# Starting the converted weight slots half a 16-byte line later in SBUF

## The chip, the cores and the metric

The kernel runs on one core of one Trainium2 chip. The metric is device time of one execution in microseconds. Three runs of the kernel before gave 966.22, 966.21 and 966.04 us, with a median of 966.21 us. The profiled execution has a span of 963.2 us from its first to its last instruction.

## The reference

The input is a sequence of 256 tokens with 1024 features, in float32. Three layers act on it one after another:

- an HGRN2 layer (a projection of 1024 to 4096 columns, a chunked gated recurrence over 8 heads, an output projection) and a squared-ReLU MLP of width 4096;
- a differential-attention layer with shared keys and values and a relative bias, and a second MLP of the same kind;
- a layer that mixes low-rank attention with a short gated convolution (three taps), a gated SiLU MLP of width 2816, and a sigmoid gate on a projected side input.

Every layer has RMS norms before and after its parts. In time it is nearly all matrix products of the form

```python
u = jax.nn.relu(h @ w_up)
return (u * u) @ w_down
```

with about 163 MB of float32 weights that are each read once.

## The kernel before, in words

**Precision scheme.** Each float32 weight and each float32 activation is split in a high part (rounded to the type fp32r, which the multiplier takes in one pass) and a low part (the rest). A product is then three fp32r matmuls: high times high, high times low, low times high. So each piece of weights is loaded into TensorE's array several times.

**Weight stream.** Weights come as "units" of 256 output columns, each in two parts of 128 x 1024 numbers (4 KB per partition). SyncE issues one DMA per part into `w_raw` (4 slots). ScalarE copies `w_raw` to `w_hi` (line 1424, rounding to fp32r). VectorE subtracts and writes `w_lo` (line 1990). `w_hi` and `w_lo` have 5 slots each (line 116). TensorE reads them in `quantum`, `high_records` and `low_records`. The semaphores `hi_ready`, `lo_ready` and `w_used` order this: a conversion waits for a slot that TensorE has done with, and SyncE's next load waits for the low part.

**Matmuls.** Mostly the weights are the stationary operand (128 columns for each load) and the activations (`xs`, `us`, `xs_b`, `xs_m`, `xs_s`) are streamed past them, 256 columns at a time (lines 657, 660, 609, 610, 617, 676 to 678, 682 to 684) or 512 at a time, high and low half together (line 649). In a few units ("tok", lines 689 to 691 and 695 to 697) the activation is stationary and the weights are streamed. Each matmul instruction has its own weight load (LDWEIGHTS) in front of it. The loads run ahead, beside the matmul before them.

**SBUF addresses.** Everything lies at hand-made addresses, one tensor after another, each rounded up to 64 bytes, from a base that is a multiple of 64. The order is `w_raw` (16,384 bytes per partition), `w_hi` (20,480), `w_lo` (20,480), `h`, a gap of 64 bytes, `xs`, a gap of 64 bytes, `mo`, `sq` and the rest, and last an arena in which the tensors of the layers (such as `us`) overlay each other. With respect to a period of 128 bytes `w_raw`, `w_hi` and `w_lo` begin at 0, and `xs` and the arena at 64, counted from the base. Each slot (4096 bytes) and each weight tile (512 bytes) is a whole number of such periods.

**Around the stream** there are RMS norms between the layers (`sums`, two or one true float32 matmuls), the recurrence's level products (lines 904 to 936, true float32), attention score products, and transposes (such as lines 843, 882, 1046).

Of the kernel before, what the change touches and what calls it, by code (L numbers as in the profile page):

```python
# [9 lines left out]
F32R = mybir.dt.float32r  # L10
# [7 lines left out]
P = 128  # L18
# [97 lines left out]
RAWS, SLOTS = 4, 5  # L116
QCOLS = 1024
HALF_PERIOD = 64
OTHER_BANKS = [PAIR0[x] + 2 for x in ("up0", "b_out", "up1", "out2", "gu", "pg")]


def pset_of(p):
    return 3 if p in OTHER_BANKS else p % 2

# [104 lines left out]
def layered_kernel(nc, a, out):  # L229

    ctx = ExitStack()
    with ctx:
# [3 lines left out]
        def sb_at(name, shape, dt, at):  # L236
            return nc.alloc_sbuf_tensor_at(name, shape, dt, offset=at)

        def sb(name, shape, dt=F32):
            size = 4 * int(np.prod(shape[1:]))  # L240
            t = sb_at(name, shape, dt, top[0])
            top[0] += (size + 63) // 64 * 64
            return t


        w_raw = sb("w_raw", [P, RAWS, QCOLS])
        w_hi = sb("w_hi", [P, SLOTS, QCOLS], F32R)
        w_lo = sb("w_lo", [P, SLOTS, QCOLS], F32R)
        h = sb("h", [P, KT, S])
        top[0] += HALF_PERIOD  # L250
        xs = sb("xs", [P, KT, 2 * S], F32R)
        top[0] += HALF_PERIOD
        mo = sb("mo", [P, KT, S])
# [207 lines left out]
        def wait(e, s, v):  # L461
            if not isinstance(v, int) or v > 0:
                e.wait_ge(s, v)
# [136 lines left out]
        def _(pe):  # L600
# [141 lines left out]
            def stream(name, x, kinds=("feat",), per=1, pairs=4, body_pairs=2, last_kt=KT - 1, waits=None,  # L742
# [6 lines left out]
                def body(i):  # L749
# [6 lines left out]
                    for b in range(body_pairs):  # L756
                        pr = i * body_pairs + b + p0
                        pset = pset_of(pr)

                        if pr - 2 in OTHER_BANKS:  # L760
                            wait(pe, pair_summed, pr - 3)
# [2297 lines left out]
```

How the kernel before makes its waits and increments, by code:

```python
        def wait_tile(e, r, t):  # L457
            e.wait_ge(h_tile, KT * r + t + 1)
# [1 line left out]
        def wait(e, s, v):  # L461
            if not isinstance(v, int) or v > 0:
                e.wait_ge(s, v)
# [11 lines left out]
        @block.sync  # L475
# [45 lines left out]
            def i_and_g(i):
                for j in range(2):
                    for part in range(2):
                        load("i0", (2, i), j, part, rows(a["a_w_in"][0], 4 * P * part, 4, 256 * (2 * i + j) + 2 * D, 256))
            times(4, i_and_g)
            square("a_out", a["a_w_out"][0], 4)
            square("up0", a["mlp_w_up"][0], 16)
            deep("down0", a["mlp_w_down"][0])
            sp.wait_ge(rel_out, 16)
            sp.wait_ge(w_used, 2 * UNIT0["up0"])
            sp.dma_start(hankel[:, :, :], bass.AP(rel_dram.tensor, rel_dram.offset, [[1, P], [REL, 16], [1, S]]))\
                .then_inc(hankel_in, 16)
# [48 lines left out]
                                 rows(a["w_down_2"][0], (8 * j + 4 * part) * P, nk, 256 * (2 * i + half), 256),  # L583
                                 nk * 256)
            times(2, down2)
            square("pg", a["w_ple_gate_2"][0], 4)
            for m in range(2):
                sp.wait_ge(row_copied[0], m + 1)
                sp.dma_start(out[0, m * P:(m + 1) * P, 0:512], rowbuf[:, m, 0:512]).then_inc(out_done, 16)
            sp.wait_ge(row_copied[2], 1)
# [3 lines left out]
            sp.wait_ge(row_copied[2], 2)  # L594
            sp.dma_start(out[0, P:S, 768:D], rowbuf[:, 1, 768:D]).then_inc(out_done, 16)
            sp.wait_ge(out_done, 80)
```

## Time and profile before

| | |
|---|---|
| median of three runs | 966.21 us |
| span of the profiled execution | 963.2 us |
| difference of the two (what lies around the span) | 3.0 us |
| TensorE matmul busy | 952.3 us (99%), 7530 instructions |
| TensorE weight load busy | 909.1 us (94%), 7530 instructions |
| VectorE busy | 748.2 us (78%) |
| ScalarE busy | 547.7 us (57%) |
| DMA | 173 GB/s mean |
| granted TensorE clock | full speed in all 40 slices |

Busy time of an engine is the union of its instructions. For matmuls it says only that one or more were under way: they are pipelined, each lasts 276 ns or more, and a new one starts every 113 ns or so. What a matmul costs is therefore read from the distance between two starts, not from its duration.

### The profile page before, as it was taken

To read this page: it belongs to the slowest core of one execution; us is meant where nothing else is said; L and a number is where in the kernel's file an instruction comes from. 1 tells how busy PE (TensorE), PEld (TensorE's weight loads), DVE (VectorE), ACT (ScalarE), POOL (GpSimd) and SP (SyncE) were. 2 spreads that over 40 slices of the span, in tenths; PEclk is the share of its full clock that TensorE was granted. 3 is DMA by queue.
4 is the path that set the end of the run, shared out by engine and by line. 5 is a ranking of instruction groups with operands and counts; after the bars stand their busy time and mean duration, and the time that the engine had idled before them with its cause. 6 is when DMAs were issued, how large, how long until landed. Compare 5 with 4: busy or idle time off the path is not lost.

```text
span 963.2 us, 18430 instructions
## 1 busy us (share of the span) xinstructions
PE 952.3 (99%) x7530; PEld 909.1 (94%) x7530; DVE 748.2 (78%) x1129; ACT 547.7 (57%) x819; POOL 89.4 (9%) x91
## 2 busy tenths in 40 slices
PE   9999999999999999999999999999999999999998
PEld 8999999999999998999999999999999999999998
DVE  6998778978855599867987844489887998787777
ACT  6652366656454476756665544455666665556455
POOL 5334101000201000001000201001001000000000
PEclk9999999999999999999999999999999999999999
DMA  8733444766666836436476575626636467665651
GB/s 256 243 120 115 143 128 140 218 200 197 195 183 193 267 109 197 150 113 183 136 215 197 176 214 184 194 68 182 183 110 202 127 197 214 187 190 170 203 175 44
DMA packets 164723, 166.62 MB, mean 173 GB/s; under 512 B 6784, under 2 KB 162832, under 8 KB 164640
## 3 DMA queue, kind: packets, MB, share of 16 engines
q1 hardware_dynamic: 162752, 163.47, 55.5%
q0 software_dynamic: 1056, 1.19, 0.5%
q8 instruction: 60, 0.98, 0.4%
q10 hardware_dynamic: 832, 0.79, 0.4%
q14 instruction: 23, 0.19, 0.1%
HBM read 163.82 MB, written 1.08 MB: 171 GB/s over the span
## 4 chain that ended last, share of the span: by engine, by line
PE 82%; DVE 12%; issue 2%; ACT 2%; DMA 2%; SPq 0%; POOL 0%; ACTq 0%; DVEq 0%
PE ps L657 19%; PE ps L660 16%; PE ps L649 13%; DVE w_lo L1990 4%; PE ps L676 3%; PE ps L677 3%; PE ps L678 3%; PE ps L682 2%; PE ps L683 2%; PE ps L684 2%; PE ps L689 2%; PE ps L609 2%; PE ps L617 2%; PE ps L690 2%; PE ps L691 2%
## 5 line engine op out<-in xcount | busy, mean ns | idle before, releaser
L1990 DVE TENSOR_TENSOR w_lo<-w_raw,w_hi 128x1024 fp32r<-128x1024 f32 (+4 forms) x314 | 375.0, 1205 | 116.1 <-ACT w_hi L1424 110.3
L1424 ACT ACTIVATE w_hi<-w_raw 128x1024 fp32r<-128x1024 f32 x298 | 313.3, 1056 | 200.3 <-PE ps L660 47.6
L657 PE MATMUL ps<-xs,w_hi 128*128 128x256 f32 x1012 | 132.6, 277 | 0.0
L657 PEld LDWEIGHTS ps<-xs,w_hi 128*128 128x128 f32 x1012 | 127.0, 188 | 4.5
L660 PE MATMUL ps<-xs,w_lo 128*128 128x256 f32 x832 | 112.2, 277 | 0.0
L660 PEld LDWEIGHTS ps<-xs,w_lo 128*128 128x128 f32 x832 | 102.9, 188 | 0.2
L682 PE MATMUL ps<-xs,w_hi 128*128 128x256 f32 x320 | 91.4, 285 | 0.4 <-DVE w_lo L1990 0.4
L683 PE MATMUL ps<-xs,w_hi 128*128 128x256 f32 x320 | 89.3, 279 | 0.0
L684 PE MATMUL ps<-xs,w_lo 128*128 128x256 f32 x320 | 89.3, 279 | 0.0
L649 PE MATMUL ps<-xs,w_hi 128*128 128x512 f32 x326 | 85.1, 393 | 0.3 <-DVE mo L2018 0.2
L1431 ACT ACTIVATE tmp<-ps 128x512 f32<-128x512 f32 x75 | 44.5, 593 | 70.6 <-PE ps L649 62.6
L657 PE MATMUL ps<-us,w_hi 128*128 128x256 f32 x626 | 81.9, 277 | 0.0
L657 PEld LDWEIGHTS ps<-us,w_hi 128*128 128x128 f32 x626 | 78.6, 188 | 2.8
L2018 DVE TENSOR_TENSOR mo<-ps,tmp 128x512 f32<-128x512 f32 x75 | 51.6, 688 | 37.1 <-ACT tmp L1431 37.0
L2968 POOL TENSOR_TENSOR sq<-sq 128x512 f32<-128x512 f32 x12 | 20.1, 1676 | 546.0 <-ACT sq L1482 375.6
L660 PE MATMUL ps<-us,w_lo 128*128 128x256 f32 x516 | 69.3, 277 | 0.0
L649 PEld LDWEIGHTS ps<-xs,w_hi 128*128 128x128 f32 x326 | 56.6, 188 | 9.8 <-DVE mo L2018 1.5
L660 PEld LDWEIGHTS ps<-us,w_lo 128*128 128x128 f32 x516 | 63.6, 188 | 0.0
L682 PEld LDWEIGHTS ps<-xs,w_hi 128*128 128x128 f32 x320 | 60.1, 188 | 0.9 <-DVE w_lo L1990 0.6
L683 PEld LDWEIGHTS ps<-xs,w_hi 128*128 128x128 f32 x320 | 60.1, 188 | 0.2
L684 PEld LDWEIGHTS ps<-xs,w_lo 128*128 128x128 f32 x320 | 60.0, 188 | 0.0
L649 PE MATMUL ps<-us,w_hi 128*128 128x512 f32 x203 | 53.4, 395 | 0.0
(431 smaller groups left out, 1896.6 us busy)
## 6 DMA issues: line engine op xcount, KB each, us to landing
w_raw<-in_mlp_w_up SPq DMA_DIRECT2D x64, 512.0 KB, 4.2
w_raw<-in_mlp_w_down SPq DMA_DIRECT2D x64, 512.0 KB, 3.5
w_raw<-in_a_w_in SPq DMA_DIRECT2D x32, 512.0 KB, 4.3
w_raw<-in_w_gate SPq DMA_DIRECT2D x22, 512.0 KB, 3.8
w_raw<-in_w_up SPq DMA_DIRECT2D x22, 512.0 KB, 4.6
w_raw<-in_w_down SPq DMA_DIRECT2D x20, 512.0 KB, 4.4
w_raw<-in_w_kv SPq DMA_DIRECT2D x16, 512.0 KB, 4.3
w_raw<-in_w_in SPq DMA_DIRECT2D x16, 512.0 KB, 3.9
```

The costliest lines, as they stand in the source:

```text
L649: o = mm(ps[:, 2 * pset + n, :], hi[:, kk, n * P:(n + 1) * P], x[:, kt0 + kk, :], start=kt0 + kk == 0, stop=kt0 + kk == last_kt)
L657: mm(ps[:, 2 * pset + n, at], hi[:, kk, n * P:(n + 1) * P], x[:, kt0 + kk, at], start=False, stop=False)
L660: o = mm(ps[:, 2 * pset + n, 0:S], lo[:, kk, n * P:(n + 1) * P], x[:, kt0 + kk, 0:S], start=False, stop=False)
L676: mm(ps[:, bank, 0:S], hi[:, kk, w], x[:, kt, 0:S], start=first, stop=False)
L677: mm(ps[:, bank, 0:S], hi[:, kk, w], x[:, kt, S:2 * S], start=False, stop=False)
L682: mm(ps[:, pset, at], hi[:, kk, w], x[:, kt, 0:S], start=first and n == 0, stop=False)
L683: mm(ps[:, pset, at], hi[:, kk, w], x[:, kt, S:2 * S], start=False, stop=False)
L684: o = mm(ps[:, pset, at], lo[:, kk, w], x[:, kt, 0:S], start=False, stop=last and n == 1)
L1424: o = fn(dst, raw, ACT.Copy)
L1431: o = fn(tmp[0:rows_, pset if slot is None else slot, :, :], ps[0:rows_, 2 * pset:2 * pset + 2, S:2 * S], ACT.Copy, scale=scale)
L1990: return v.tensor_tensor(d, x, y, ALU.subtract)
L2018: return v.tensor_tensor(dst, ps[0:rows_, 2 * pset:2 * pset + 2, 0:S], tmp[0:rows_, pset if slot is None else slot, :, :], ALU.add)
```

## The change

`w_hi` and `w_lo` are each allocated as one flat run that is 128 bytes longer than before. A view of it that starts two float32 elements (8 bytes) in takes the place of the old tensor. All instructions, waits and slot numbers stay as they are. By the allocation the tensors move like this:

- `w_hi` begins 8 bytes later;
- `w_lo` begins 136 bytes later (128 for the longer `w_hi`, and 8);
- all tensors behind them, `h` and `xs` to the arena, begin 256 bytes later and keep their place in a period of 128 bytes;
- `w_raw` stays where it is.

A 16-byte line holds four float32 numbers. Before, each weight tile of 128 columns lay on 32 whole lines. After, it lies on 31 whole lines and two half ones.

```diff
 HALF_PERIOD = 64
+HALF_LINE = 2
...
         w_raw = sb("w_raw", [P, RAWS, QCOLS])
-        w_hi = sb("w_hi", [P, SLOTS, QCOLS], F32R)
-        w_lo = sb("w_lo", [P, SLOTS, QCOLS], F32R)
+
+        def shifted(t, n):
+            return t[:, HALF_LINE:HALF_LINE + n * QCOLS].rearrange("p (s n) -> p s n", s=n)
+
+        w_hi = shifted(sb("w_hi", [P, SLOTS * QCOLS + 2 * HALF_PERIOD // 4], F32R), SLOTS)
+        w_lo = shifted(sb("w_lo", [P, SLOTS * QCOLS + 2 * HALF_PERIOD // 4], F32R), SLOTS)
         h = sb("h", [P, KT, S])
         top[0] += HALF_PERIOD
         xs = sb("xs", [P, KT, 2 * S], F32R)
```

## Rows read from the trace of the kernel before

**Rows 1.** The page: the span, busy time of each engine, the chain that ended last

```profile
span 963.2 us, 18430 instructions
...
PE 952.3 (99%) x7530; PEld 909.1 (94%) x7530; DVE 748.2 (78%) x1129; ACT 547.7 (57%) x819; POOL 89.4 (9%) x91
...
PE 82%; DVE 12%; issue 2%; ACT 2%; DMA 2%; SPq 0%; POOL 0%; ACTq 0%; DVEq 0%
```

**Rows 2.** Groups of instructions: busy us, mean ns of one, idle before

```profile
L1990 DVE TENSOR_TENSOR w_lo<-w_raw,w_hi 128x1024 fp32r<-128x1024 f32 (+4 forms) x314 | 375.0, 1205 | 116.1 <-ACT w_hi L1424 110.3 <-ACT w_hi L1418 1.5 <-DVE hq_both L2264 0.2
L1424 ACT ACTIVATE w_hi<-w_raw 128x1024 fp32r<-128x1024 f32 x298 | 313.3, 1056 | 200.3 <-PE ps L660 47.6 <-PE ps L649 38.0 <-PE ps L691 27.1
L649 PE MATMUL ps<-xs,w_hi 128*128 128x512 f32 x326 | 85.1, 393 | 0.3 <-DVE mo L2018 0.2
L689 PE MATMUL ps<-w_hi,xs 128*128 128x256 f32 x128 | 37.2, 290 | 0.0
```

**Rows 3.** Line 1990 by itself: who waited for it (us, times)

```profile
L1990 DVE TENSOR_TENSOR w_lo<-w_raw,w_hi x314: 219/1224/2325, 13.2 to 949.8; 128x1024 fp32r<-128x1024 f32 x149, 128x64 fp32r<-128x64 f32 x2, 128x128 fp32r<-128x128 f32 x2, 128x512 fp32r<-128x512 f32 x2
...
  PEld ps L682: 0.6, 1
  PE ps L682: 0.4, 1
  PEld ps L1143: 0.4, 1
  PE ps L1143: 0.2, 1
```

**Rows 4.** Timeline, matmuls, 12.75 to 13.6 us: start us, duration us

```profile
12.75 0.28 PE L683 MATMUL ps<-xs,w_hi 128*128 128x256 f32 x1
...
13.10 0.28 PE L683 MATMUL ps<-xs,w_hi 128*128 128x256 f32 x1
...
13.45 0.28 PE L683 MATMUL ps<-xs,w_hi 128*128 128x256 f32 x1
```

**Rows 5.** Timeline, matmuls, 616.7 to 617.6 us

```profile
616.75 0.28 PE L676 MATMUL ps<-us,w_hi 128*128 128x256 f32 x1
...
617.09 0.28 PE L676 MATMUL ps<-us,w_hi 128*128 128x256 f32 x1
...
617.43 0.28 PE L676 MATMUL ps<-us,w_hi 128*128 128x256 f32 x1
```

**Rows 6.** Stretches: length, busy us and instructions of each engine, PEclk, DMA, GB/s

```profile
345.00:360.00 15.00, 15.00 (x128) 14.95 (x127) 14.70 (x26) 12.85 (x22) 1.58 (x1) 1.00 0.29 97
612.00:630.00 18.00, 18.00 (x161) 18.00 (x160) 9.06 (x8) 7.94 (x9) 0.00 (x0) 1.00 0.55 154
10.00:22.00 12.00, 12.00 (x104) 12.00 (x103) 11.82 (x18) 9.61 (x15) 4.03 (x6) 1.00 0.95 288
783.60:930.00 146.40, 146.40 (x1140) 140.21 (x1139) 113.24 (x130) 81.91 (x103) 2.23 (x2) 1.00 0.66 198
```

**Rows 7.** Timeline, matmuls, 958 to 958.8 us: weights streamed, activation stationary

```profile
958.15 0.28 PE L695 MATMUL ps<-w_hi,xs 128*128 128x256 f32 x1
...
958.50 0.28 PE L695 MATMUL ps<-w_hi,xs 128*128 128x256 f32 x1
```

**Rows 8.** Lines 657 and 676 by themselves: ns min/median/max by moving tensor

```profile
L657 PE MATMUL ps<-xs_m,w_hi x34: 276/279/365, 720.4 to 736.0; 128*128 128x256 f32 x34
L657 PE MATMUL ps<-xs_b,w_hi x18: 279/279/280, 441.8 to 444.8; 128*128 128x256 f32 x18
...
L676 PE MATMUL ps<-xs_b,w_hi x16: 279/279/283, 446.5 to 451.8; 128*128 128x256 f32 x16
...
L676 PE MATMUL ps<-xs_m,w_hi x16: 276/276/276, 737.7 to 742.8; 128*128 128x256 f32 x16
```

**Rows 9.** Timeline, weight loads of 64-column matmuls, 52.4 us

```profile
52.36 1.87 PEld L936 LDWEIGHTS ps<-hq_both,hk 128*128 128x128 f32 x16
```

**Rows 10.** Timeline, weight loads of line 917: moving operand from a line start, from a half line

```profile
77.87 1.90 PEld L917 LDWEIGHTS ps<-hq_both,hk 128*128 128x128 f32 x16
...
82.57 1.89 PEld L917 LDWEIGHTS ps<-hq_both,hk 128*128 128x128 f32 x16
```

**Rows 11.** VectorE lines 2749 and 2108: ns min/median/max

```profile
L2749 DVE SCALAR_TENSOR_TENSOR cy<-cx,vec,cy x8: 476/481/484, 686.7 to 707.2; 128x255 f32<-128x255 f32 x4, 128x254 f32<-128x254 f32 x4
...
L2108 DVE SCALAR_TENSOR_TENSOR mo<-mo,vec,rstd x42: 470/479/485, 159.8 to 941.8; 128x256 f32<-128x256 f32 x42
```

## The prediction

> **What bounds the kernel now.** I read the page first. TensorE is busy for 952.3 of 963.2 us, and the chain that ended last is 82% PE [rows 1]. VectorE has 12% of the chain, but it is not a second bound: over the whole run TensorE and its weight loads waited for a `w_lo` for 1.6 us in all, against 375 us of work in that line [rows 2, 3]. VectorE itself sat idle for 116 us in front of these subtractions and ScalarE for 200 us in front of its copies [rows 2]. So the kernel is worth what TensorE's stream of matmuls is worth. The reader is to see there that a busy share of 99% doesn't say how fast the stream runs. For that I went to the timeline and took the distances between starts.
>
> They come in two paces. At 12.75 us the same line starts again after three matmuls, at 13.10 and at 13.45: 0.35 us for three, 117 ns each [rows 4]. At 616.75 us it is 617.09 and 617.43: 0.34 for three, 113 ns each [rows 5]. Over longer stretches of 256-column matmuls alone: 15.00 us with 128 of them is 117.2 to 118.1 ns (by 128 or 127 intervals), 18.00 us with 161 is 111.8 to 112.5, where both ends of a stretch cut a pipelined instruction [rows 6]. From the single starts in the timeline I get 117.8 and 113.3 ns. Counted over the run, about 2,450 of the 256-column matmuls start at the slow pace and about 3,600 at the fast one.
>
> What sets the pace? Not the clock: PEclk is 1.00 in stretches of both kinds, at either pace it is the upper of its two levels, 2.4 GHz [rows 6]. Not the line of code or the operand: line 657 has 276 ns for one with `xs_m` and 279 with `xs_b` and line 676 the same, 276 and 279 [rows 8]. The duration carries the pace in it, as the rows of either pace show. Not who else works: VectorE is busy 98% of the time in a slow stretch and 50% in the fast one of rows 6, but it is also busy 77% of the time in the 146 us from 783.6 on, all of them at the fast pace [rows 6]. The pace holds for 50 to 600 matmuls at a time and changes only at a break, so it is a locked rhythm of weight load and matmul. What locks it the rows don't show. This is the part of the kernel that an address could touch.
>
> **The change part by part.**
>
> *ScalarE's copies*, 298 with 1056 ns, now write from a half line. The row of a copy between whole lines is all there is [rows 2]. If each took one more step of its stream (1 ns) it would be 0.3 us in 963, and 4 ns each 1.2 us, hidden under 200 us of idle time. A gain is bounded in the same way. I take 0, ends -0.3 and +0.3 on the span.
>
> *VectorE's subtractions*, 314, read one operand from a line start and one from a half line, and write from a half line. The convolution's taps have that form. Line 2749 reads `cx` from its start, and reads and writes `cy` from its first or second element on. With 254 and 255 columns it takes 481 ns, the aligned 256-column form of line 2108 takes 479 [rows 11]. For 254 columns I would expect 2 ns less than for 256, so at most 4 ns is due to the start. 314 x 4 ns = 1.3 us on VectorE, under 116 us of idle time, with TensorE waiting 1.6 us in all [rows 2, 3]. On the span: 0, ends -0.1 and +0.3.
>
> The Trainium skill has a rule that agrees (Vector Engine (DVE) Microarchitecture Reference, Measured stream behaviour on trn2): a port streams at full rate in runs of at least two neighbouring words that start on an 8-byte boundary, and 8 bytes is what the change moves. By it the price is 0, as by the row.
>
> *Streamed weights* (lines 689 to 691, 695 to 697, and line 649's form for a few; 444 matmuls in all by the timeline) now stream from a half line. They run at the same 117 ns as other lines do in the slow pace [rows 4, 7]. The nearest row of a moving operand that starts at a half line is the second of rows 10: in line 917 the level products stream pairs of numbers from every second half line, and 16 weight loads take 1.89 us there, against 1.90 us for the sixteen whose operand starts on a line. So 0. But the pace of those may be that of the load. The upper end is a line's worth of columns, 4 x 0.44 ns = 1.8 ns, x 444 = 0.8 us.
>
> *Weight loads from a half line* are the main term: 5,682 for 256-column matmuls and 567 for 512-column ones, counted in the timeline. No row shows a load from a half line. First, does their length matter? The matmuls of line 936 stream only 64 columns, and still 16 loads take 1.87 us, (1.87 - 0.19) / 15 = 112 ns from start to start [rows 9]. So a load of 128 columns has a pace of its own of 112 ns, 0.875 ns per column, and the fast pace of 113.3 is 1.3 ns above it. Anything up to 1.3 ns more per load can vanish, anything beyond it is paid in full. Lower end: 0. Upper end: one line's worth of columns, 4 x 0.875 = 3.5 ns, 2.2 ns beyond the cover, x 5,682 = 12.5 us (and 19.9 us if there is no cover). The loads for 512 columns lie under 393 ns matmuls [rows 2] and cost nothing. I take 0: nearest is the row of the same engine with the other operand [rows 10], and on VectorE too the half line is free [rows 11].
>
> The Trainium skill speaks for and against this (SBUF — State Buffer, Specifications, and its note on cachelines): SBUF has 16-byte lines, full bandwidth needs at least two hits on a line, and "each access that crosses to a new line pays a penalty". By the first half a half line with its two hits is free. By the second, 33 lines are touched in place of 32, and each load pays once more. That reading is the second rival below, whose price is made from rows. No row of before has an operand of weights at a half line, so the trace doesn't decide it.
>
> *The two paces.* If they depend on where weights and activations lie relative to each other, 8 bytes can move the point at which a break drops the stream in one or the other. All at the fast pace: 2,450 x 4.45 ns = 10.9 us less. All at the slow pace: 3,600 x 4.45 = 16.0 us more. I take 0. Moving and stationary operands change roles in the "tok" lines, `xs` stationary and `w_hi` streamed, and the slow pace there is the same 117 ns [rows 4, 7]; if relative position made the pace, swapping it should show.
>
> *The rest moves by 256 bytes*, and `w_lo` against `w_hi` by 128. The loads never use both at once, and each keeps its place in a period of 128 bytes apart from the 8. 0, with no bound of its own beside the two paces.
>
> The sum: span 963.2 + 0, and 3.0 us around it, so the median again, 966.2 us. For scale, a measurement of this kernel can tell about 0.2%, 1.9 us, from no change.
>
> **The rivals.**
>
> *A. The paces shift in its favour.* For it: 2,450 matmuls, 40% of them, run at the slow pace, so there is much to win. The pace changes at breaks, so a small push can last for hundreds of matmuls. Against it: roles swapped, same paces [rows 4, 7]. All of it would be 955.3 us. Half is the likelier size, 5.4 us: 960.8 us.
>
> *B. Each load pays for the extra line* (the slower side). Place: 5,682 loads in front of 256-column matmuls. Price: 2.2 ns each beyond the 1.3 ns of cover [rows 5, 9]. It decides from 1.3 ns per load on, and passes what can be told from no change at 1.7 ns. Full: 966.2 + 12.5 = 978.7 us. For it: the load is what sets the fast pace, it has next to no slack. Against it: half-line starts are free in both places where a row has one [rows 10, 11].
>
> *C. The paces shift against it.* The mirror of A: 3,600 fast matmuls could fall to the slow pace. The long fast stretches, like those 146 us [rows 6], make a full loss unlikely. A third is 5.3 us: 971.5 us.
>
> *D. The change doesn't do what it says.* If the base weren't a multiple of 16 bytes, the old slots would have been off a line already. The allocation rounds to 64, so this has next to no chance, and its time is that of no change.
>
> **How the numbers follow.** No effect (with D) 0.47, A 0.24, B 0.14, C 0.15. The likeliest has a range of its own of 965.5 to 967.0 us: the bounds of the ScalarE, VectorE and streamed terms together. The range that should hold the time 8 times in 10 is 960.5 to 974.0 us. It leaves out the larger half of A, about 0.09, and of B the part above 1.4 ns beyond the cover, with C's tail about 0.11. Faster by over 0.2%: A with little cut off, 0.24. Within 0.2%: 0.47. Slower by over 0.2%: B and C, 0.29.
>
> **What the changed profile would show.** If I am right: distances of 113 and 118 ns in the same stretches as before, weight loads of 188 ns, subtractions of 1224 ns, and a span within 1 us of 963.2. B shows in the fast stretches, at 616 us for instance, as starts more than 113.3 ns apart, 115.5 at its full price, and in every one of them alike. A and C leave 113 and 118 ns alone and change how many there are of each: the stretch of 345 to 360 us would hold more than 128 matmuls, or that of 612 to 630 fewer than 161. My forecast fails if any of these moves by more than 1%. If VectorE's line 1990 rises from 1224 ns by more than 10, the row of the taps misled me, though the time should not follow. A third pace, neither 113 nor 118, would show that the address sets the rhythm itself, and that my argument from the swapped roles was wrong.

## The result, and the profile after

The changed kernel takes 984.13 us (median; 984.1 to 984.45) against 966.12 us for the kernel before: 1.9% slower, ratio 1.0189 with a 95% interval of 1.0175 to 1.0204. The forecast was 966.2 us, with a range up to 974.0. It was wrong: the measured time lies 10.1 us above the range.

The page, first, answers to [rows 1]. The span has grown by 19.1 us, and TensorE's busy time with it by 19.3. VectorE (748.2 to 748.8) and ScalarE (547.7 to 549.2) have the same work as before:

```profile
span 982.3 us, 18430 instructions
...
PE 971.6 (99%) x7530; PEld 927.6 (94%) x7530; DVE 748.8 (76%) x1129; ACT 549.2 (56%) x819; POOL 89.6 (9%) x91
...
PE 86%; DVE 10%; issue 2%; ACT 1%; DMA 1%; POOL 0%; ACTq 0%; DVEq 0%
```

The groups that touch the slots answer to [rows 2]. Line numbers are 5 higher. Columns: busy us, mean ns of one, idle before:

```profile
L1995 DVE TENSOR_TENSOR w_lo<-w_raw,w_hi 128x1024 fp32r<-128x1024 f32 (+4 forms) x314 | 375.2, 1206 | 127.5 <-ACT w_hi L1429 124.6 <-ACT w_hi L1423 1.5
L1429 ACT ACTIVATE w_hi<-w_raw 128x1024 fp32r<-128x1024 f32 x298 | 313.6, 1057 | 212.3 <-PE ps L665 57.3 <-PE ps L654 41.7 <-PE ps L696 28.2
```

A subtraction takes 1206 ns (before 1205) and a copy 1057 (1056). The half-line start costs these two engines 1 ns at most. What grew is the idle time in front of them, by 11 and 12 us: the subtractions wait for the copies, and the copies for a slower TensorE.

The timeline of the stretch that answers to [rows 5] (the same matmuls, now at 629 us; start us, duration us):

```profile
629.00 0.28 PE L681 MATMUL ps<-us,w_hi 128*128 128x256 f32 x1
629.12 0.28 PE L682 MATMUL ps<-us,w_hi 128*128 128x256 f32 x1
629.24 0.28 PE L683 MATMUL ps<-us,w_lo 128*128 128x256 f32 x1
629.35 0.28 PE L681 MATMUL ps<-us,w_hi 128*128 128x256 f32 x1
...
629.71 0.28 PE L681 MATMUL ps<-us,w_hi 128*128 128x256 f32 x1
```

Three matmuls took 0.34 us before, now 0.35 to 0.36. From the single starts of all 172 threes on `us`, the three lines are on average 119.2, 116.7 and 117.6 ns apart from the next, where it was 113.3 for all three together. The stretches that answer to those of [rows 4, 6] at the slow pace:

```profile
10.00:22.00 12.00, 12.00 (x104) 12.00 (x103) 11.93 (x19) 9.94 (x15) 4.06 (x6) 1.00 0.92 288
352.00:367.00 15.00, 15.00 (x128) 14.95 (x127) 14.70 (x26) 12.80 (x21) 1.59 (x1) 1.00 0.34 103
```

There were 104 matmuls from 10 to 22 us before and there are 104 now, and 128 in the 15 us after 345, now after 352. Over all matmuls with starts 112.5 to 135 ns apart (6,120 before, 6,116 after) the mean went from 115.18 to 118.19 ns: 3.0 ns x 6,116 = 18.4 us. PEclk is 1.00 in both, so it is not the clock.

Both traces have the same 7530 matmuls in the same order, so each can be set against its own former self. The 3,579 that ran at the fast pace went from 113.3 to 118.2 ns on average, which is 17.4 us. The 2,441 at the slow pace went from 117.8 to 118.2 ns, 0.9 us. The 512-column ones went from 229.4 to 231.6 ns, 1.2 us. So nearly the whole loss is that the fast pace is gone. What took its place is not the old slow pace: single distances now spread from 115 to 123 ns. In the text below, a series is 14 or more 256-column matmuls without a break, and its average leaves out the first three. The kernel before has 156 series, and 3,534 of its matmuls stand in series that average 113.3 to 113.7 ns. The changed kernel also has 156, and the fastest of them averages 115.5 ns.

### The profile page after: what moved, and what is told of

The parts are those of the page before. It is cut to its first block, busy times and chain, and to the rows that moved or that the text cites. A ratio compares the mean times of both kernels' runs of the same rounds, so it can differ in the third digit from the quotient of the medians.

```text
span 982.3 us, 18430 instructions
## 1 busy us (share of the span) xinstructions
PE 971.6 (99%) x7530; PEld 927.6 (94%) x7530; DVE 748.8 (76%) x1129; ACT 549.2 (56%) x819; POOL 89.6 (9%) x91
## 3 DMA queue, kind: packets, MB, share of 16 engines
q0 software_dynamic: 1056, 1.19, 0.5%
## 4 chain that ended last, share of the span: by engine, by line
PE 86%; DVE 10%; issue 2%; ACT 1%; DMA 1%; POOL 0%; ACTq 0%; DVEq 0%
PE ps L662 20%; PE ps L665 17%; PE ps L654 13%; DVE w_lo L1995 3%; PE ps L681 3%; PE ps L682 3%; PE ps L683 3%; PE ps L687 2%; PE ps L688 2%; PE ps L689 2%; PE ps L622 2%; PE ps L614 2%; PE ps L615 2%; PE ps L694 2%; PE ps L696 2%
## 5 line engine op out<-in xcount | busy, mean ns | idle before, releaser
L1995 DVE TENSOR_TENSOR w_lo<-w_raw,w_hi 128x1024 fp32r<-128x1024 f32 (+4 forms) x314 | 375.2, 1206 | 127.5 <-ACT w_hi L1429 124.6
L1429 ACT ACTIVATE w_hi<-w_raw 128x1024 fp32r<-128x1024 f32 x298 | 313.6, 1057 | 212.3 <-PE ps L665 57.3
L662 PE MATMUL ps<-xs,w_hi 128*128 128x256 f32 x1012 | 136.6, 280 | 0.0
L662 PEld LDWEIGHTS ps<-xs,w_hi 128*128 128x128 f32 x1012 | 130.4, 188 | 4.5
L665 PE MATMUL ps<-xs,w_lo 128*128 128x256 f32 x832 | 116.1, 282 | 0.0
L665 PEld LDWEIGHTS ps<-xs,w_lo 128*128 128x128 f32 x832 | 106.3, 189 | 0.2
L687 PE MATMUL ps<-xs,w_hi 128*128 128x256 f32 x320 | 92.0, 287 | 0.4 <-DVE w_lo L1995 0.4
L688 PE MATMUL ps<-xs,w_hi 128*128 128x256 f32 x320 | 89.5, 280 | 0.0
L689 PE MATMUL ps<-xs,w_lo 128*128 128x256 f32 x320 | 89.5, 280 | 0.0
L662 PE MATMUL ps<-us,w_hi 128*128 128x256 f32 x626 | 84.2, 280 | 0.0
L662 PEld LDWEIGHTS ps<-us,w_hi 128*128 128x128 f32 x626 | 80.6, 188 | 2.8
L665 PE MATMUL ps<-us,w_lo 128*128 128x256 f32 x516 | 71.6, 282 | 0.0
L654 PEld LDWEIGHTS ps<-xs,w_hi 128*128 128x128 f32 x326 | 56.8, 188 | 10.2 <-DVE mo L2023 1.2
L665 PEld LDWEIGHTS ps<-us,w_lo 128*128 128x128 f32 x516 | 65.7, 189 | 0.0
L687 PEld LDWEIGHTS ps<-xs,w_hi 128*128 128x128 f32 x320 | 60.2, 188 | 0.9 <-DVE w_lo L1995 0.6
L688 PEld LDWEIGHTS ps<-xs,w_hi 128*128 128x128 f32 x320 | 60.3, 188 | 0.2
L689 PEld LDWEIGHTS ps<-xs,w_lo 128*128 128x128 f32 x320 | 60.1, 188 | 0.0
```

Source lines behind the costliest of these rows:

```text
L654: o = mm(ps[:, 2 * pset + n, :], hi[:, kk, n * P:(n + 1) * P], x[:, kt0 + kk, :], start=kt0 + kk == 0, stop=kt0 + kk == last_kt)
L662: mm(ps[:, 2 * pset + n, at], hi[:, kk, n * P:(n + 1) * P], x[:, kt0 + kk, at], start=False, stop=False)
L665: o = mm(ps[:, 2 * pset + n, 0:S], lo[:, kk, n * P:(n + 1) * P], x[:, kt0 + kk, 0:S], start=False, stop=False)
L687: mm(ps[:, pset, at], hi[:, kk, w], x[:, kt, 0:S], start=first and n == 0, stop=False)
L688: mm(ps[:, pset, at], hi[:, kk, w], x[:, kt, S:2 * S], start=False, stop=False)
L689: o = mm(ps[:, pset, at], lo[:, kk, w], x[:, kt, 0:S], start=False, stop=last and n == 1)
```

## The experiments

Starts are given in bytes in a period of 128, first of the weights (`w_hi` and `w_lo`), then of the activations. The kernel before has 0 and 64. All times are medians.

| kernel | weights | activations | us | ratio to before (95%) |
|---|---|---|---|---|
| changed | 8 | 64 | 984.1 | 1.0189 (1.0175 to 1.0204) |
| e1 padded only | 0 | 64 | 963.8 | 0.9981 (0.9972 to 0.9990) |
| e2 | 16 | 64 | 982.0 | 1.0171 (1.0156 to 1.0186) |
| e3 | 8 | 72 | 998.1 | 1.0336 (1.0318 to 1.0353) |
| e4 | 0 | 72 | 997.6 | 1.0332 (1.0317 to 1.0348) |
| e5 | 32 | 64 | 982.7 | 1.0179 (1.0163 to 1.0194) |
| e6 | 64 | 64 | 985.2 | 1.0206 (1.0191 to 1.0221) |
| e7 | 8 and 0 | 64 | 981.3 | 1.0165 (1.0148 to 1.0182) |
| e8 | 0 | 96 | 992.2 | 1.0278 (1.0263 to 1.0294) |
| e9 | 0 | 0 | 987.4 | 1.0221 (1.0205 to 1.0236) |
| e10 | 64 | 0 | 964.0 | 0.9979 (0.9969 to 0.9988) |
| e11 | 128 = 0 | 64 | 965.8 | 0.9998 (0.9988 to 1.0008) |
| e12 | 16 | 80 | 971.8 | 1.0064 (1.0049 to 1.0079) |
| e13 | 0 | 80 | 990.2 | 1.0254 (1.0237 to 1.0271) |
| e14 | 96 | 64 | 986.1 | 1.0210 (1.0195 to 1.0225) |
| e15 | 0 | 64 | 965.9 | 1.0003 (0.9993 to 1.0012) |
| e18 | 0 | 64 | 968.3 | 1.0025 (1.0016 to 1.0034) |

**First four: is it the half line?** The edits of e1 and e2, on the changed kernel:

```diff
-HALF_LINE = 2
+HALF_LINE = 0      # e1; 4 in e2
```

> The two slots are allocated 128 bytes longer as in the changed kernel, but begin at the start of their memory: w_hi where it was, w_lo 128 bytes and all behind it 256 bytes later. Theory 1 (a weight tile that starts half a line in costs its own load) and theory 2 (what counts is where weights lie relative to the streamed activations within a line or a period of 128 bytes) both expect no effect: 966 us, starts of matmuls 113.3 ns apart in the fast stretches. Theory 3 (what was moved along, by 128 and 256 bytes, made it slow) expects the changed kernel's 984 us.

> As the changed kernel, but both slots begin 16 bytes (a whole line) later instead of 8. Theory 1 (half-line start of the load) expects all of the loss gone: 966 us and 113.3 ns in the fast stretches. Theory 2 (position relative to the activations, in a period longer than a line) expects another time than 966, by more than 2 us in either direction, and another pattern of distances. Theory 2 in its narrow form (relative position within a 16-byte line) expects 966 too.

e3 (on the changed kernel) and e4 (on the kernel before) shift what is streamed by 8 bytes. `later` gives a view that starts that many elements in (cut short):

```diff
-        xs = sb("xs", [P, KT, 2 * S], F32R)
-        top[0] += HALF_PERIOD
+        xs = later(sb("xs", [P, KT * 2 * S + HALF_PERIOD // 4], F32R), [KT, 2 * S], 2)
...
-            return sb_at(name, shape, dt, arena + at)
+            return later(sb_at(name, [shape[0], size // 4 + 8], dt, arena + at), shape[1:], 2)
```

> The changed kernel, with xs and every tensor of the arena (us, xs_b, xs_m, xs_s among them) also 8 bytes later, so that weights and streamed activations again lie relative to each other as before, and all start half a line in. Theory 1 expects the loss to stay, 984 us or more, since every weight load still starts half a line in and the streamed side is off its lines too. Theory 2 expects 966 us within 2.

> The kernel before, with xs and the tensors of the arena 8 bytes later and the converted weights where they were. Theory 1 (the weight load's own start) expects 966 us, apart from 432 matmuls in which the activation is the stationary side: at most 4.5 ns each, 2 us. Theory 2 (relative position) expects a loss of the size of the change, 984 us within 6, the pattern may be the mirrored one.

e1 clears what moved along of the loss. e2 refutes theory 1: a whole line later, every load on whole lines again, costs 16 us of the 18. Theory 2 as it stood fell as well: with the distance restored (e3) the time did not come back, it rose to 998. Both operands matter, and at a start 8 bytes later the streamed one more.

**Next four: a larger piece, or the distance?** The start is 32 and 64 bytes in e5 and e6 (`HALF_LINE` of 8 and 16). e7 has `w_hi` shifted and `w_lo` not, e8 is e4 with 32 bytes.

> As the changed kernel with a start 32 bytes later. Half a line and a whole line cost nearly the same (984.1 and 982.0 us) and activations off by 8 bytes cost 998, with the weights moved along or not. Theory A (each operand pays for its own start when it isn't a multiple of a piece larger than a line): with a piece of 32 bytes 964 us, starts at 113.3 ns again; with a piece of 64 bytes 982 us. Theory B (distance between weights and activations in a period of 128 bytes, 64 apart being best) expects a smooth dependence: a distance of 32 costs more than one of 48, so over 984 us.

> As the changed kernel with a start 64 bytes later: weights and activations then have the same place in a period of 128 bytes. Theory A expects 964 us, as with a start 0 bytes later, since 64 is a multiple of 32 and of 64. Theory B expects the worst case of all starts, over 990 us.

> Only w_hi begins 8 bytes later, w_lo begins at the start of its memory (128 bytes later than in the kernel before). Two thirds of the three-pass matmuls load from w_hi. Theory A and theory B both expect two thirds of the loss of 20.4 us against the padded kernel if the loads pay one by one: 977 us, the starts after loads from w_lo at 113 to 114 ns. If instead one late load upsets the rhythm of the next ones too, more than that, up to 984 us, with no 113 ns starts left.

> The kernel before with xs and the tensors of the arena 32 bytes later, weights where they were. Theory A with a piece of 32 bytes expects 964 to 966 us; with a piece of 64 bytes a loss as large as that of 8 bytes, 990 to 998 us. Theory B expects the loss of a distance of 32 in 128, the same as in e5_weights_32, whatever that is.

Pieces of 32 and 64 bytes are out: e5 and e6 are as slow as half a line. So is the smooth form of theory B: it wanted over 984 us from e5 and over 990 from e6, and it wanted e8 to equal e5, but e8 is 9.5 us slower. e7 came out at 981.3, not 977. Its groups of matmuls on `us`:

```profile
L663 PE MATMUL ps<-us,w_hi 128*128 128x256 f32 x626 | 84.8, 282 | 0.0
L666 PE MATMUL ps<-us,w_lo 128*128 128x256 f32 x516 | 69.9, 278 | 0.0
```

in the changed kernel, where both tensors are off:

```profile
L662 PE MATMUL ps<-us,w_hi 128*128 128x256 f32 x626 | 84.2, 280 | 0.0
L665 PE MATMUL ps<-us,w_lo 128*128 128x256 f32 x516 | 71.6, 282 | 0.0
```

and before:

```profile
L657 PE MATMUL ps<-us,w_hi 128*128 128x256 f32 x626 | 81.9, 277 | 0.0
L660 PE MATMUL ps<-us,w_lo 128*128 128x256 f32 x516 | 69.3, 277 | 0.0
```

With `w_lo` back in place its group needs 69.9 us, near the 69.3 of before, and `w_hi`'s a little more than in the changed kernel. From the single starts, for all that had been fast: a `w_hi` matmul is 118.9 ns from the next, a `w_lo` one 115.8 ns, where both had 113.3 to 113.4. So most of the loss goes with the tensor that lies wrong, and a part falls on its neighbours.

**Three that settle the distance.** e9 is e4 with 64 bytes, e10 shifts both operands by 64, e11 has `HALF_LINE` of 32 (128 bytes, so the weights' place in the period is that of before).

> The kernel before with xs and the arena tensors 64 bytes later, so that activations and weights both begin at 0 in a period of 128 bytes. Any start of the weights but 0 cost 16 to 20 us (8, 16, 32 and 64 bytes alike). Theory A with a piece of 128 bytes, each operand by its own start: no loss against 965 us, or a gain, since now the activations too begin on a piece. Theory B (weights and activations must be 64 apart): a loss as in e6_weights_64, 985 us or more.

> Weights and activations both 64 bytes later: the distance between them is again that of the kernel before, the weights begin at 64 and the activations at 0 in a period of 128. Theory A with a piece of 128 expects the loss of e6_weights_64 to stay, 982 to 986 us. Theory B expects 964 to 966 us.

> As the changed kernel with a start 128 bytes later. Theory A with a piece of 128 and theory B both expect the time of the padded kernel, 964 us, within 3. If not, the period is 256 bytes or more, and w_hi or w_lo pays: 970 to 985 us.

This is the clean result of the study. Weights 64 later: 985. Activations 64 later: 987. Both: 964. A place in a period of 128 bytes that is bad for one operand is made good by moving the other. And 128 bytes later the time is that of before. The groups on `us` of e10 show the fast pace back, with 276 ns for one:

```profile
L671 PE MATMUL ps<-us,w_hi 128*128 128x256 f32 x626 | 81.5, 276 | 0.0
L674 PE MATMUL ps<-us,w_lo 128*128 128x256 f32 x516 | 68.9, 276 | 0.0
```

The single starts say the same of every kernel on the table. At any distance but 64 (changed, e2, e4 to e9, e13, e14), none of the 155 or 156 series of a kernel averages under 115 ns, whatever ran before it. At distance 64 on the starts 0 and 64 (before, e1, e10, e11, e15, e18), 3,500 to 4,500 matmuls stand in series of 113.2 to 113.7 ns. With half-line starts at that distance (e3), no series is under 119.5 ns.

**Four for what was left.** e12 and e13 shift both operands and the activations alone by 16 bytes, e14 the weights by 96. e15 is the padded kernel with another 128 bytes in front of `xs`:

```diff
-        top[0] += HALF_PERIOD
+        top[0] += 3 * HALF_PERIOD
         xs = sb("xs", [P, KT, 2 * S], F32R)
```

> Weights and activations both 16 bytes (a whole line) later, 64 apart in 128 as in the kernel before. With both 8 bytes later it was 998 us, with both 64 later 964. If the 998 us were the price of half-line starts, this costs nothing: 964 to 966 us. If a start must be a multiple of 32 or 64 bytes whatever the distance, 980 us or more.

> Only the activations 16 bytes later: distance 80 in 128, all on whole lines. Theory B (a distance other than 64 costs 16 to 20 us, and more where the activations are ahead) with a half-line price for streamed operands expects 982 to 992 us, under the 998 of activations 8 bytes later. If half lines have no price of their own it should be near 998 too.

> Weights 96 bytes later: the distance from weights to activations is 96 in 128, the same as with activations 32 bytes later (992 us). If the distance alone counts among whole-line starts: 992 us within 3. If the weights' own start or their distance to something else counts, more like the 982 of weights 32 later.

> The padded kernel (964 us) with xs and all behind it another 128 bytes later: places in a period of 128 bytes unchanged, in 256 changed. A try at a faster one. If only 128 counts, 964 us within 2; if 256 counts for the share of matmuls in the slow pace, between 955 and 970 us.

With the distance kept, whole-line starts cost 972 (e12) and half-line starts 998 (e3), so half a line has a price when both operands are on it: 26 us. For streamed operands alone it comes to 7 us (e4 against e13), for weights alone to 2 us (changed against e2). These two pairs also differ by 8 bytes of distance, all of them bad ones, so they are no clean prices. e12's 6 us over before were not forecast by either theory. Its trace has no series under 114.2 ns: most of those that had run at 113.3 run at 114.5 to 114.8, and one of 192 matmuls at 118.3. e14 is 6 us under e8 at the same distance, between the two times that its expectation named: the own start has a smaller say besides the distance.

e15's time shows no gain, but its stream got faster. From 10 to 22 us it holds 108 matmuls, where before, in [rows 6], it had 104:

```profile
10.00:22.00 12.00, 12.00 (x108) 12.00 (x107) 11.93 (x20) 10.00 (x16) 4.04 (x6) 1.00 0.93 279
```

Of some 6,020 matmuls of 256 columns on the converted weights, 2,441 started 116 ns or more apart in the kernel before, and 1,028 in e15. (In e11 it was 1,073, in e1 1,414, in e10 1,445.) Set against before one by one, the 256-column matmuls of e15 took 5.9 us less. The 512-column ones took 1.7 us more, at 232.4 ns for 229.4, and the rest, mostly pauses in which TensorE waits for others, 4.7 us more. In e11 the pause that grew most was a wait for a `w_lo`, 1.6 us where it had been 0.4. So more than half of the slow pace did go away, and its gain was spent on slower 512-column matmuls and on waits.

**TensorE alone.** e16 is a program of its own, with no work for VectorE or ScalarE during the blocks. In each block of 72 the order of loads and streams is that of the three-pass matmuls (shortened; `tile of i` and `half of i` stand for the index arithmetic):

```python
for x in STARTS:            # streamed operand: 0, 4, 8, 16, 32, 64, 96 bytes
    for y in STARTS:        # stationary operand
        for i in range(72):
            mm(ps[:, 0, 0:256], w[y][:, tile of i], a[x][:, half of i], start=True, stop=True)
        plain_mms(2)
```

> None of the reference's computation: TensorE alone runs 49 blocks of 72 fp32r matmuls of 256 columns, each with its load of 128, for all pairs of starts 0, 4, 8, 16, 32, 64 and 96 bytes (in a period of 128) of stationary (w) and streamed (a) operand; between blocks two small float32 products; the output is zeros. No other engine or transfer is active. If the loss is made by TensorE's two reads against each other, the two pairs of starts 0 and 64 (either way round) stand out at 113 to 114 ns per matmul (8.1 to 8.2 us of starts per block), pairs with equal starts need 118 to 120 (8.5 us), and a streamed operand at 8 bytes is the slowest with 120 or more. If it takes ScalarE's and VectorE's accesses to the slots, all 49 blocks have the same pace.

Some of its groups of 72. Busy time less the last matmul's own 0.28 us, over 71, is about the distance of starts:

```profile
L72 PE MATMUL ps<-a_thirtytwo,w_ninetysix 128*128 128x256 f32 x72 | 8.4, 277 | 0.0
L72 PE MATMUL ps<-a_sixtyfour,w_zero 128*128 128x256 f32 x72 | 8.7, 280 | 0.0
L72 PE MATMUL ps<-a_sixtyfour,w_eight 128*128 128x256 f32 x72 | 8.7, 280 | 0.0
L72 PE MATMUL ps<-a_sixtyfour,w_sixtyfour 128*128 128x256 f32 x72 | 8.9, 284 | 0.0
L72 PE MATMUL ps<-a_eight,w_zero 128*128 128x256 f32 x72 | 8.9, 284 | 0.0
L72 PE MATMUL ps<-a_four,w_four 128*128 128x256 f32 x72 | 9.0, 287 | 0.0
```

All distances, ns from start to start in the timeline, without the first six of each block (columns: start of the stationary operand; the first block began at the lower clock level, with 213 ns, and is left out):

```
streamed at     0       4       8      16      32      64      96
 0             --   118.4   115.5   118.3   118.3   117.8   117.3
 4          123.4   122.2   120.2   122.1   120.7   121.6   120.0
 8          120.0   120.0   120.1   120.0   120.9   120.0   120.0
16          116.7   117.8   119.8   118.3   117.2   119.2   119.3
32          116.7   120.0   117.8   120.0   119.9   118.3   113.3
64          117.8   117.8   116.7   116.7   116.7   120.0   118.3
96          120.0   117.8   120.0   118.1   117.8   116.6   120.0
```

From 60 to 460 us the profile has no VectorE or ScalarE instruction and a DMA share of 0.00, and the dependence is there: TensorE alone is enough to make it. One pair of 48 runs at 113.3 ns, and its distance is 64. Equal starts on whole lines cost 118.3 to 120.0. A streamed operand at half a line costs 120.0 to 120.9 whatever the weights do, one at a single word 120 to 123. But my expectation failed in part: the pairs of 0 and 64, either way, ran at 117.8. That is the slow pace of the kernel before. Each pair has one block here, with one way in, so differences of a few ns within the table can't be put down to the addresses alone.

e17 therefore holds the distance at 64 and changes the way in, through none, 3 or 6 matmuls of 512 columns after the two plain ones:

```diff
-                    plain_mms(2)
+                    plain_mms(2)
+                    wide_mms(wide, x, y)
```

> None of the reference's computation: TensorE alone, only pairs of starts 64 bytes apart (in a period of 128): streamed operand at 64, 0, 96, 32, 72, 8, 80, 16 with the stationary one at 0, 64, 32, 96, 8, 72, 16, 80. Each pair has three blocks of 72 matmuls of 256 columns, entered after two small float32 products alone, or after these and 3 or 6 matmuls of 512 columns. If a distance of 64 has two paces whichever start it has and the way in decides, each pair on whole lines shows 113.3 or 117.8 ns and nothing else, and the entries over 512 columns give 113.3 more often. If a start that is no multiple of 32 bars the fast pace, the pairs at 16 and 80 show no 113.3 in any of their blocks, which would explain the 972 us of both operands 16 bytes later. The pairs at 8 and 72 show 119 to 121 in all blocks.

The timeline of the matmuls (each row a whole block; start us, duration us):

```profile
43.79 8.21 PE L81 MATMUL ps<-a_sixtyfour,w_zero 128*128 128x256 f32 x71
...
52.97 8.65 PE L81 MATMUL ps<-a_sixtyfour,w_zero 128*128 128x256 f32 x72
...
63.29 8.64 PE L81 MATMUL ps<-a_sixtyfour,w_zero 128*128 128x256 f32 x72
...
81.54 8.34 PE L81 MATMUL ps<-a_zero,w_sixtyfour 128*128 128x256 f32 x72
...
109.80 8.65 PE L81 MATMUL ps<-a_ninetysix,w_thirtytwo 128*128 128x256 f32 x72
...
120.12 8.33 PE L81 MATMUL ps<-a_ninetysix,w_thirtytwo 128*128 128x256 f32 x72
...
166.51 8.81 PE L81 MATMUL ps<-a_seventytwo,w_eight 128*128 128x256 f32 x72
...
225.26 8.33 PE L81 MATMUL ps<-a_eighty,w_sixteen 128*128 128x256 f32 x72
```

A block of 8.33 to 8.34 us is 113.3 ns from start to start once it has settled ((8.34 - 0.28) / 71 = 113.5 with the slower entry), 8.64 to 8.65 is 117.8, 8.81 is 120. So the same addresses show both paces with the same instructions and operands inside the block, and only what ran before it differs: streamed at 64 and stationary at 0, the first block is fast, the next two slow. That entries over 512 columns help was wrong for this pair. Starts at 16 and 80 reach 113.3 too, so with TensorE alone the own start doesn't bar the fast pace, which I had offered as the reason of e12. With half-line starts no block got below 120.0.

In e17 the pairs with the stationary operand 64 bytes behind the streamed one, at the higher place (streamed/stationary 0/64, 32/96, 16/80), all ended fast, and five of nine blocks with it 64 ahead did not (all tensors there begin at a multiple of 256). But e16 had a block against this already: streamed at 0, stationary at 64, it stayed at 117.8 ns to its end. e18 tries this order in the kernel: kernel before, `xs` and all behind it 128 bytes later, the same line as in e15.

> The kernel before with xs and all behind it 128 bytes later, one number changed. In a period of 256 bytes both kinds of weights then begin 64 bytes behind the activations; in the kernel before it is 64 ahead, and in the kernels at 964 to 966 us one of w_hi and w_lo was on either side. With TensorE alone all eight blocks with the stationary operand 64 bytes behind the streamed one ended at 113.3 ns, whatever their way in (on whole lines), and of nine with it 64 ahead five stayed at 117.8 or more. If that holds in the kernel, most of its 2,450 slow matmuls become fast: 956 to 961 us. If the order in 256 bytes doesn't count here: 964 to 966 us.

It failed: 968.3 us, slower by 0.25%. The groups on `us`, wide and narrow, before and in e18:

```profile
L649 PE MATMUL ps<-us,w_hi 128*128 128x512 f32 x203 | 53.4, 395 | 0.0
L676 PE MATMUL ps<-us,w_hi 128*128 128x256 f32 x172 | 47.5, 276 | 0.0
...
L649 PE MATMUL ps<-us,w_hi 128*128 128x512 f32 x203 | 54.1, 397 | 0.0
L676 PE MATMUL ps<-us,w_hi 128*128 128x256 f32 x172 | 48.3, 281 | 0.0
```

The 512-column matmuls are 3 ns slower each (232.4 for 229.4 ns from start to start), and line 676 fell to the slow pace. Other stretches became fast: 1,987 matmuls start 116 ns or more apart, for 2,441 before. One by one, the 256-column matmuls took 1.9 us less, the 512-column ones 1.7 us more and the pauses 3.1 us more. The order in 256 bytes shows most plainly in the 512-column matmuls, nearly all of which load from `w_hi`: among the kernels with starts of 0 and 64 they take 232.4 ns in the three with `w_hi` behind (e11, e15, e18) and 229.1 to 229.4 ns in the three with it ahead (before, e1, e10).

## Why the prediction was wrong

- **What bounds the kernel, two paces, no clock in it:** right. The loss is in TensorE's distances between starts, and the slow stretches of before lost next to nothing (117.8 to 118.2 ns). Two readings on the way were off. Line 657 has a median of 279 ns with `xs_m` too, 276 is its least [rows 8], so that row doesn't show one line at two paces. And the pace of before lasts for 22 matmuls in places, for over 1,000 in others, not for 50 to 600.
- **ScalarE's copies and VectorE's subtractions, 0:** right, 1057 and 1206 ns for 1056 and 1205.
- **Weight loads from a half line, 0 with ends of 0 and +12.5 us (19.9 without cover):** the wider end is near the 18 us measured, but by luck, for its reason is wrong. Loads on whole lines 16, 32, 64 or 96 bytes later cost the same 982 to 986 us. Half a line in place of a whole one is 2 us of the 18 (changed against e2, both at a bad distance).
- **The two paces, "I take 0":** this is the step that failed. The argument was that "tok" matmuls swap the roles, with `xs` stationary and `w_hi` streamed, and keep their paces, so relative position could not count. But 64 bytes in a period of 128 is its own mirror: swapped, the distance is 64 again. The row could not tell the two cases apart. What the runs showed in its place: distance 64 is what permits the fast pace, and any other takes it away (985 us with the weights 64 later, 987 with the activations, 964 with both). The term's own upper bound, all 3,600 matmuls of the fast pace dropping to the slow one for 16.0 us, is close to the 17.4 us that they did lose. But rival C was priced at a third of it, on the argument that long fast stretches make a full loss unlikely, and the range stopped at 974. C also had matmuls move between 113 and 118 ns, while they left both. The text named the right sign for this, a third pace, though what came is a spread of 115 to 123 ns.
- **Streamed weights, 0, upper end 0.8 us:** mis-sized. In line 694 one takes 294 ns for 290 before, and in lines 694 to 696 it is 119.7 to 121.4 ns from start to start for 116.4 to 116.5, 4 ns x 444 = 1.8 us. One by one, the 432 of 256 columns took 1.4 us more. Not all of it need be the half line, since a whole line later (e2) they took 0.9 us more. With TensorE alone a streamed operand at half a line ran at 120.0 to 120.9 against all starts of the other. The row from line 917 misled as the prediction itself had warned: 16 loads in 1.89 us, 113 ns each, is near the load's own 112 and can hide what the stream costs.
- **Rival B, each load pays for an extra line, 978.7 us, 0.14:** right in sign and in where it shows (in every fast stretch alike), wrong in size (118 ns, not 115.5) and in mechanism: e2 puts each load back on 32 whole lines and keeps the loss. It was the place where a rule was cited. The Trainium skill (SBUF — State Buffer, its note on cachelines) asks for two or more hits on a line for full bandwidth, which two numbers on a half line give, and names a penalty for each new line; neither says that the distance of two operands counts. The half-line runs of VectorE (1206 ns for 1205) and ScalarE (1057 for 1056) agree with the first half. For TensorE's streamed operand e16 and e17 do not: no block with it at a half line ran under 120.0 ns, while whole-line blocks reached 113.3. The measurement decides.
- **The rest moves by 256 bytes and `w_lo` by 128, 0:** nearly. e1 holds these moves alone, and they gained 0.2%. So the change's other 8 bytes cost some 20 us, not 18.

Not settled: why a distance of 64 is the good one, what in the way in locks the stream into either pace, and why whole-line starts at 16 and 80 run at 114.5 ns or more in the kernel though 113.3 is open to them with TensorE alone. e10 and e1 beat the kernel before by 0.2%, at 964.0 and 963.8 us. e15 and e11 got rid of more than half of the slow pace but gained no time by it; no run got rid of all of it.

## What to carry to other kernels

Where TensorE streams fp32r with a load for every 256 columns, treat the addresses of its two operands as one choice. Here starts of 0 and 64 in a period of 128 were worth 1.6 to 3.4% against every placement tried with another distance or half-line starts, and 0.6% against 16 and 80; it can be tried by moving one tensor. Read the pace from the distance between starts; a busy share of 99% looked the same at 966 and at 984 us. When the stream gets faster and the time does not, as in e15, look for the waits that grew. And before a row is taken as evidence against a dependence, check that the row differs in the thing at issue: a swap leaves a distance of half the period as it was.

## What the runs showed of the hardware that I had not expected

- The addresses of TensorE's two operands count jointly. With TensorE alone the distance between starts went from 113.3 to 123.4 ns with nothing but the starts of its operands changed (e16).
- With the streamed operand at 64 and the stationary one at 0, and with 96 and 32, there are two rhythms for one and the same code and addresses, 113.3 and 117.8 ns, and either lasted through a block of 72 (e17). In the kernel before both lasted through series of over 100 matmuls.
- A streamed operand 4 or 8 bytes off its line costs 120 ns or more in nearly every pair, and a stationary one in that place as little as 115.5 ns (streamed at 0, stationary at 8).
- The 512-column matmuls tell apart places that are the same in a period of 128 bytes: 232.4 ns with `w_hi` 64 behind the activations in a period of 256, 229.1 to 229.4 ns with it 64 ahead.
